# Up to four units of an expert at a time: their up projections first, then their down projections

## The reference

```python
for e in range(N_EXPERTS):
    gu = t @ w_up[e] + b_up[e]
    glu = jnp.minimum(gu[:, 0::2], SWIGLU_LIMIT)
    lin = jnp.clip(gu[:, 1::2], -SWIGLU_LIMIT, SWIGLU_LIMIT)
    act = glu * jax.nn.sigmoid(SWIGLU_ALPHA * glu) * (lin + 1.0)
    y = y + combine[:, e:e + 1] * (act @ w_down[e] + b_down[e])
```

## Time and profile before

| | us |
|---|---|
| median of 3 runs | 1302.47 (1299.08 to 1303.08) |
| the profiled execution | 1299.44 |
| its span, first to last instruction | 1297.7 |
| TensorE matmuls busy | 1116.5 (86% of the span) |
| VectorE busy | 417.1 (32%) |
| ScalarE busy | 219.0 (17%) |
| mean rate over the span | 367 GB/s, 475.76 MB |

### The profile page before, as it was taken

The page is one execution under the profiler, slowest core; times in us unless marked ns, Lnnn a source line. Parts: engine busy times, 40 slices in busy tenths (PEclk is TensorE's granted clock), DMA queues, the critical chain, the costliest instruction groups (busy, mean ns, idle before and its releaser), DMA issues.

```text
span 1297.7 us, 19403 instructions
## 1 busy us (share of the span) xinstructions
PE 1116.5 (86%) x7944; PEld 480.3 (37%) x7944; DVE 417.1 (32%) x1144; ACT 219.0 (17%) x461; POOL 42.2 (3%) x75
## 2 busy tenths in 40 slices
PE   6999998899989556669999667979679797999996
PEld 5864466788533111113333112323213231333331
DVE  1489988641142111112232111322112121232231
ACT  1121023630131000001112100111001110111210
POOL 2000000055000000000000000000000000000000
PEclk9999999999989988889999879998989798999998
DMA  9997771356859999999999999999999999599997
GB/s 327 361 373 300 261 258 65 131 169 219 327 229 428 427 427 428 428 427 428 428 428 427 427 427 427 425 427 427 427 428 428 427 428 428 233 422 423 424 428 312
DMA packets 65561, 475.76 MB, mean 367 GB/s; under 512 B 6329, under 2 KB 18942, under 8 KB 38878
## 3 DMA queue, kind: packets, MB, share of 16 engines
q1 hardware_dynamic: 61844, 471.36, 88.5%
q0 software_dynamic: 816, 1.97, 0.6%
q10 hardware_dynamic: 2842, 1.56, 0.4%
HBM read 473.03 MB, written 1.05 MB: 365 GB/s over the span
## 4 chain that ended last, share of the span: by engine, by line
PE 56%; DMA 33%; DVE 4%; ACT 3%; SPq 3%; issue 1%; ACTq 0%; another core or an unknown queue 0%; DVEq 0%
DMA weights<-in_w_up 19%; PE bank L1549 16%; DMA weights<-in_w_down 14%; PE bank L1577 9%; PE bank L1279 6%; PE bank L1286 5%; PE bank L1491 5%; SPq L458 3%; PE bank L1222 2%; PE bank L1478 2%; PE bank L1271 2%; PE bank L1424 2%; DVE weights L854 2%; PE bank L1498 1%; PE bank L1192 1%; ACT buf_d L768 1%
## 5 line engine op out<-in xcount | busy, mean ns | idle before, releaser
L1549 PE MATMUL bank<-weights,buf_d 128*32 128x512 f32 x3008 | 391.6, 667 | 135.9 <-DMA weights<-in_w_up 135.9
L1549 PEld LDWEIGHTS bank<-weights,buf_d 128*32 128x32 f32 x3008 | 96.2, 116 | 407.6 <-DMA weights<-in_w_up 205.7
L1577 PE MATMUL bank<-weights,buf_d 128*32 128x512 f32 x1504 | 173.6, 596 | 11.5 <-DMA weights<-in_w_down 8.3
L1163 DVE TENSOR_SCALAR u_conv<-bank 128x256 f32<-128x256 f32 x47 | 20.0, 425 | 455.9 <-PE bank L1549 455.9
L764 ACT ACTIVATE u_conv<-u_conv 128x256 f32<-128x256 f32 x47 | 19.6, 416 | 665.6 <-DVE u_conv L1163 665.6
L1491 PE MATMUL bank<-buf_d 64*128 64x512 f32 x384 | 99.9, 640 | 0.9 <-DVE buf_d L1175 0.9
L854 DVE SCALAR_TENSOR_TENSOR weights<-u_conv,weights 128x256 f32<-128x256 f32 x240 | 97.7, 479 | 0.5
L1577 PEld LDWEIGHTS bank<-weights,buf_d 128*32 128x32 f32 x1504 | 42.8, 109 | 108.5 <-issue 74.5
L1279 PE MATMUL bank<-weights,buf_d 128*128 128x512 f32 x192 | 82.9, 593 | 0.0
L1175 DVE TENSOR_TENSOR buf_d<-bank,u_conv 128x512 f32<-128x512 f32 x47 | 32.5, 692 | 144.9 <-PE bank L1577 144.9
L1491 PEld LDWEIGHTS bank<-buf_d 64*128 64x128 f32 x384 | 35.3, 199 | 74.8 <-issue 74.8
(11 more groups left out here) (273 smaller groups left out, 823.3 us busy)
## 6 DMA issues: line engine op xcount, KB each, us to landing
weights<-in_w_up SPq DMA_DIRECT2D x128, 2048.0 KB, 34.1
weights<-in_w_down SPq DMA_DIRECT2D x64, 2048.0 KB, 36.9
weights<-in_w_in SPq DMA_DIRECT2D x10, 2048.0 KB, 14.1
weights<-in_w_ada SPq DMA_DIRECT2D x8, 2048.0 KB, 18.2
weights<-in_w_ada SPq DMA_DIRECT2D x8, 1024.0 KB, 11.5
weights<-in_w_in SPq DMA_DIRECT2D x8, 512.0 KB, 10.4
weights<-in_w_in SPq DMA_DIRECT2D x4, 1024.0 KB, 12.9
weights<-in_w_conv_out SPq DMA_DIRECT2D x2, 2048.0 KB, 11.6
```

Source lines behind the costliest of these rows:

```text
L1549: ins = t.matmul(UP[SLOTS * g:SLOTS * g + SLOTS, :], xgT[:, r, SLOTS * j:SLOTS * j + SLOTS], up_group(w[:, r, :], g), start=False, stop=(j ...
L1577: ins = t.matmul(DOWN[rows, :], actT[:, r, at:at + SLOTS], w[:, g, r, NB * i:NB * i + NB], start=(r == 1 and h == 0 and g == 0), stop=(h = ...
```

## The change

The units of an expert go in runs of up to four (QUEUE). Within a run all up parts come first, one behind the other, and then all down parts. TensorE's up part holds the bias rows, c0 and c1, the gather of the next unit, c2, the transposes of the gathered tokens, c3. Its down part holds the transposes of pickw and of act, the combine of the previous unit, the bias rows and c4 and c5. The products lin of a run wait in four tiles of 256 columns (queue); ScalarE copies them one by one into act in the down part. The sigmoid is written over its own input glu, and so starts behind the product of lin and glu. sel exists twice, for up and for down. apply_mod goes in two halves, four operations for two, the first half after c1 is used. VectorE's and ScalarE's programs get a copy of the loops for every expert, as TensorE's has. The core of the diff:

```diff
+QUEUE = 4
...
-        act = area_q[:, 512:768]
-        actT = area_q[:, 768:1024].rearrange("p (r s) -> p r s", r=2)
-        xg = area_q[:, 1024:1280]
+        queue = area_q[:, 512:512 + QUEUE * T]
+        actT = area_q[:, 1792:2048].rearrange("p (r s) -> p r s", r=2)
+        xg = area_q[:, 1536:1792]
...
-        oe = area_q[:, 1536:2048]
+        oe = area_k[:, 848:848 + NB]
...
-        sel = area_k[0:3 * EXPERTS, 576:576 + SLOTS // 2].bitcast(BF16)
+        sel_up = area_k[0:3 * EXPERTS, 576:576 + SLOTS // 2].bitcast(BF16)
+        sel_down = area_k[0:3 * EXPERTS, 2146:2146 + SLOTS // 2].bitcast(BF16)
         glu = area_k[:, 592:848]
         comb4 = glu.rearrange("p (k e) -> p k e", e=EXPERTS)
-        lin = area_k[:, 848:1104]
-        sg = area_k[:, 1104:1360]
+        act = glu
...
+        up_pairs = UP[:, :].rearrange("p (f two) -> p f two", two=2)
+
+        def expert_end(eng, e):
+            return eng.value_load(unit_ends[0:1, e:e + 1], min_val=e + 1, max_val=UCOLS - 1)
+
+        def run_end(first, end):
+            n = (end - first).with_bounds(min_val=1, max_val=T // SLOTS)
+            more = ((n - 1) >> 2).with_bounds(min_val=0, max_val=1)
+            return (first + (n - more * (n - QUEUE)).with_bounds(min_val=1, max_val=QUEUE)).with_bounds(min_val=1, max_val=UCOLS - 1)
+
+        def queued(u, first):
+            return queue[:, bass.ds((u - first).with_bounds(min_val=0, max_val=QUEUE - 1) * T, T)]
...
             g.memset(oe, 0.0).then_inc(oe_ready, 1)
+            g.memset(queue[:, 3 * T:4 * T], 0.0).then_inc(up_read, 1)
...
-            count = act_e.value_load(unit_ends[0:1, EXPERTS - 1:EXPERTS], min_val=EXPERTS, max_val=UCOLS - 1)
-            with act_e.Fori(0, count) as u:
-                act_e.wait_ge(glu_ready, u + 1)
-                s.activation(sg, glu, ACT.Sigmoid, scale=ALPHA).then_inc(sg_ready, 1)
+
+            def up_part(u, first):
                 act_e.wait_ge(gathered, u + 2)
                 s.copy(xg, GX[:, 0:T]).then_inc(xs_ready, 1)
+                act_e.wait_ge(glu_read, u + 1)
+                s.activation(glu, glu, ACT.Sigmoid, scale=ALPHA).then_inc(sg_ready, 1)
+                act_e.wait_ge(act_ready, u + 1)
+
+            def down_part(u, first):
+                s.copy(act, queued(u, first)).then_inc(act_kept, 1)
                 act_e.wait_ge(t_done, u + 1)
                 s.copy(actT, TR[:, 0:T].rearrange("p (r s) -> p r s", r=2)).then_inc(actT_ready, 1)
+                act_e.wait_ge(cmb_read, u + 1)
                 s.copy(Cmb, TR[:, T:2 * T]).then_inc(cmb_ready, 1)
+
+            begin = 0
+            for e in range(EXPERTS):
+                end = expert_end(act_e, e)
+                with act_e.Fori(begin, end, QUEUE) as first:
+                    last = run_end(first, end)
+                    with act_e.Fori(first, last) as u:
+                        up_part(u, first)
+                    with act_e.Fori(first, last) as u:
+                        down_part(u, first)
+                begin = end
...
-            def apply_mod(link, at, done):
...
+            def apply_mod(link, at, half, done):
+                pair = slice(2 * half, 2 * half + 2)
...
+                link(v.tensor_tensor(to, seen, xg_scale[:, :, pair].unsqueeze(3).to_broadcast(places), ALU.mult), at)
+                v.tensor_tensor(to, to, xg_shift[:, :, pair].unsqueeze(3).to_broadcast(places), ALU.add).then_inc(done, 1)
 
             dve.wait_ge(xt_done, 1)
-            apply_mod(lambda ins, at: step(ins), 0, xm_ready)
+            apply_mod(lambda ins, at: step(ins), 0, 0, xm_low)
+            apply_mod(lambda ins, at: step(ins), 0, 1, xm_ready)
...
+            def make_sel(dst, u, ready):
+                v.tensor_copy(dst, onehot[:, bass.ds(u, 1)].to_broadcast([3 * EXPERTS, SLOTS])).then_inc(ready, 1)
+
+            def make_pickw(u):
...
+
+            make_pickw(0)
+            PER_UNIT = 2
+
+            def up_part(u, first):
+                def link(ins, k):
+                    ins.then_inc(u_step, 1)
+                    dve.wait_ge(u_step, u * PER_UNIT + k)
+
+                lin = queued(u, first)
                 make_pick(u + 1)
+                dve.wait_ge(xt_done, u + 2)
+                dve.wait_ge(chunk_used[1], u + 1)
+                apply_mod(link, 1, 0, xm_low)
                 dve.wait_ge(UP_DONE, u + 1)
-                pairs = UP[:, :].rearrange("p (f two) -> p f two", two=2)
-                v.tensor_scalar(glu, pairs[:, :, 0], LIMIT, None, ALU.min).then_inc(glu_ready, 1)
-                link(v.tensor_scalar(lin, pairs[:, :, 1], LIMIT, -LIMIT, ALU.min, ALU.max), 1)
+                v.tensor_scalar(glu, up_pairs[:, :, 0], LIMIT, None, ALU.min).then_inc(glu_ready, 1)
+                v.tensor_scalar(lin, up_pairs[:, :, 1], LIMIT, -LIMIT, ALU.min, ALU.max).then_inc(up_read, 1)
+                apply_mod(link, 2, 1, xm_ready)
                 dve.wait_ge(glu_ready, u + 1)
-                link(v.scalar_tensor_tensor(lin, lin, 1.0, glu, ALU.add, ALU.mult), 2)
+                dve.wait_ge(up_read, u + 2)
+                v.scalar_tensor_tensor(lin, lin, 1.0, glu, ALU.add, ALU.mult).then_inc(glu_read, 1)
+                make_sel(sel_up, u + 1, sel_up_ready)
                 dve.wait_ge(sg_ready, u + 1)
-                v.tensor_tensor(act, lin, sg, ALU.mult).then_inc(act_ready, 1)
-                dve.wait_ge(gathered, u + 2)
-                make_sel(u + 1)
-                dve.wait_ge(xt_done, u + 2)
-                apply_mod(link, 3, xm_ready)
-
+                v.tensor_tensor(lin, lin, glu, ALU.mult).then_inc(act_ready, 1)
+
+            def down_part(u):
+                dve.wait_ge(t_done, u + 1)
+                make_pickw(u + 1)
                 dve.wait_ge(DOWN_DONE, u + 1)
                 v.tensor_tensor(oe, DOWN[:, :], gate2, ALU.mult).then_inc(oe_ready, 1)
+                make_sel(sel_down, u + 1, sel_down_ready)
+
+            begin = 0
+            for e in range(EXPERTS):
+                end = expert_end(dve, e)
+                with dve.Fori(begin, end, QUEUE) as first:
+                    last = run_end(first, end)
+                    with dve.Fori(first, last) as u:
+                        up_part(u, first)
+                    with dve.Fori(first, last) as u:
+                        down_part(u)
+                begin = end
...
-            def unit(e, u):
+            def up_rows(e, j):
+                w = up_chunk(e, j)
+                pe.wait_ge(w_full[chunk_slot(e, j)], chunk_landed(e, j))
+                for r in range(2):
+                    for g in range(GROUPS):
+                        ins = t.matmul(UP[SLOTS * g:SLOTS * g + SLOTS, :], xgT[:, r, SLOTS * j:SLOTS * j + SLOTS],
+                                       up_group(w[:, r, :], g), start=False, stop=(j == 3 and r == 1))
+                ins.then_inc(chunk_used[j], 1)
+
+            def up_part(e, u):
+                pe.wait_ge(xm_low, u + 1)
+                pe.wait_ge(sel_up_ready, u + 1)
+                pe.wait_ge(up_read, u + 1)
+                bias_rows(UP, range(GROUPS), sel_up, up_bias)
+                up_rows(e, 0)
+                up_rows(e, 1)
                 pe.wait_ge(xm_ready, u + 1)
-                pe.wait_ge(sel_ready, u + 1)
-                bias_rows(UP, range(GROUPS), up_bias)
-                for j in range(4):
-                    w = up_chunk(e, j)
-                    pe.wait_ge(w_full[chunk_slot(e, j)], chunk_landed(e, j))
-                    for r in range(2):
-                        for g in range(GROUPS):
-                            ins = t.matmul(UP[SLOTS * g:SLOTS * g + SLOTS, :], xgT[:, r, SLOTS * j:SLOTS * j + SLOTS],
-                                           up_group(w[:, r, :], g), start=False, stop=(j == 3 and r == 1))
-                    ins.then_inc(chunk_used[j], 1)
-
-                pe.wait_ge(oe_ready, u + 1)
-                pe.wait_ge(cmb_ready, u + 1)
-                combine()
-                pe.wait_ge(units_ready, 2)
-                bias_rows(DOWN, (0, 2), down_bias)
                 pe.wait_ge(pick_ready, u + 2)
                 gather()
+                up_rows(e, 2)
+                pe.wait_ge(xs_ready, u + 2)
+                transpose_halves(GX, T, xg).then_inc(xt_done, 1)
+                up_rows(e, 3)
+
+            def down_part(e, u):
                 pe.wait_ge(pickw_ready, u + 1)
+                pe.wait_ge(cmb_ready, u + 1)
                 for tt in range(TT):
                     t.transpose(TR[:, T + P * tt:T + P * tt + P], pickw[:, tt, :], ident[:])
-                pe.wait_ge(act_ready, u + 1)
+                pe.wait_ge(act_kept, u + 1)
                 transpose_halves(TR, 0, act).then_inc(t_done, 1)
-                pe.wait_ge(xs_ready, u + 2)
-                transpose_halves(GX, T, xg).then_inc(xt_done, 1)
-
+                pe.wait_ge(oe_ready, u + 1)
+                combine(read=cmb_read)
+                pe.wait_ge(sel_down_ready, u + 1)
```

(25 more changed lines are left out.)

21 lines of the change are left out of this document (5 added, 16 removed).

## The result

The changed kernel takes 1336.5 us (median of four runs, 1333.8 to 1338.9) against 1301.0 before (four runs), a ratio of 1.027, with 1.024 to 1.030 as its 95% interval. The forecast was 1331, slower with a chance of 0.92. Direction, mechanism and range held; the long wait and the unit's own time were a little too small, and two statements about the DMA were wrong.

The account below looks back on a forecast made before the run. Expert weight transfers and TensorE were all but level, with TensorE becoming the bound from unit 34: 33.7 us of waits plus 9 of lower clock less 14.1 gained gives +28.6, hence 1331 us; range 1315 to 1350.

Parts of the forecast that it names:

- (a): Joint from up part to down part, once per expert: TensorE waits 3.1 us ahead of the act transposes, seven times.
- The drain of the Trainium skill: Full drain after each VectorE operation would add about 9 us; the sum instead used clamps measured 0.34 us apart.
- (b): Joint from up part to up part: TensorE waits 1.9 us for the UP bank and sel_up, six times.
- (c): Joint from down part to down part: the combine waits 0.1 us for the previous unit's oe, six times.
- The clock: TensorE's lower clock level behind each 3.1 us wait: 1.3 us each, seven times, 9 us; short waits charged nothing.
- The gain of 14.1 us: From unit 34 on, TensorE free of weight waits would reach the tail at 1276.4 us instead of 1290.5.
- No new hole there: Ahead of unit 34, units 8 to 15: TensorE falls back 22 us, the ring of chunks holds 25 us ahead.
- ACT_TABLE_LOAD: ScalarE's table load, 1.28 us per unit, priced at nothing: expected beneath the third and fourth chunk's rows.
- (2): Rival: the same TensorE waits, but the clock holds; +19.6 us, 1322 us, chance 0.22.
- (3): Rival: more exposed at the joints, or low clock behind short waits too; 1341 to 1350 us, chance 0.13.
- (4): Rival: waits are short and removing the transfer hole wins, long wait under 1.2 us; 1298 or 1288 us, chance 0.06.
- (5): Rival: waits at their floors of 2.0 and 0.9 us with a full clock; 1308 us or somewhat less, chance 0.04.

Follow-up runs that it names:

- fill_wait: Changed kernel plus twenty useless TensorE transposes of the identity in the long wait ahead of each run's down parts; 1324.0 us.
- all_three: Changed kernel with the combine ahead of the wait for act, sel_up made ahead of the clamps and apply_mod's high half behind the second multiply; 1312.1 us.
- the second profile: The changed kernel run and profiled once more, nothing altered; 1336.1 us in one run.
- peeled: Changed kernel with each run's first down part written out, combine first, transposing straight from the queue; sel_up early, apply_mod's high half late; 1306.6 us.
- comb_first: Changed kernel with the previous unit's combine ahead of the wait for act and its transposes in TensorE's down part; 1323.6 us.
- hi_late: Changed kernel with the high half of apply_mod moved from between the clamps and the product to behind the last multiply; 1337.7 us.
- before_loops: Kernel before, order of work unchanged, with the change's per-expert loops, value_load and run_end on VectorE, ScalarE and TensorE; 1302.0 us, ratio 1.0002.
- sel_early: Changed kernel with VectorE making sel_up for the next unit ahead of the clamps instead of behind the product; 1338.5 us.
- peeled_two: As peeled, but a run holds at most two units instead of four; 1305.0 us, ratio 1.0021.

## Why the prediction was right or wrong

**What bounds the kernel, and who takes over: right.** Behind unit 34 TensorE waits for no weights in the changed kernel. Its stretch is 185.1 + 35.5 + 13.2 us; fill_wait takes most of the last term away, all_three more than half of the second. The span grew by 10.9 us more than forecast (39.5 for 28.6): 4.9 ahead of unit 34, 1.8 in the waits, 4.2 in the rest.

**(a), the long wait: 3.1 forecast, 3.28 measured.** Up to the second multiply each step sat where the sum had it: lin at T + 0.35 (0.34), the high half at + 0.68 and + 0.99 (0.68 and 1.00), product + 1.20 (1.21), sigmoid + 1.65 (1.67), multiply + 2.10 (2.13). The step that was mis-sized is ScalarE's way from the multiply to the copy: the copy started 0.60 us after the multiply's end, where I had 0.04 + 0.25. Hand-over, the way out of one loop and into the next, and the address of the queued tile all lie in it, and no run takes them apart.

**The drain of the Trainium skill, weighed against the row.** The changed kernel's independent operations start 0.33 to 0.35 us apart (L1204, L1205, L1161), and the chain came out where the sum by the row had it. The Trainium skill ("VectorE: DVE Perf Modes", section "The DRAIN you can't avoid") has the full drain as its main case and a start earlier than that as the exception; the trace shows the exception alone, and 9 us more of drains would have been wrong.

**(b) and (c): 1.9 forecast, 1.87 measured; 0.1 forecast, 0.2 measured.**

**The clock: mechanism right, size near.** 7 x 1.3 = 9 us forecast; of the rest of 13.2 us the clock is 10.7 (against fill_wait), in the second profile 8.3 of 10.7. The forecast lies between two profiles of the same kernel, so how well it sits is in part luck. A smaller term that I missed is in the rest too: a unit at full clock takes 8.71 + 6.35 = 15.06 us without its waits, from up part to up part and down part to down part, where I used 14.91; 0.15 x 12 = 1.8. The clock is 1.2 to 1.5 us for each long wait on average, 0 in the expert that begins at 1207 us (35.54 = 2 x 15.06 + 3.28 + 1.87 + 0.23) and 1.7 in the single-unit one (20.03 - 15.06 - 3.28). The 1.9 us waits, which I charged nothing, were rightly charged nothing: no fall of the clock comes behind one.

**The gain of 14.1 us: the number held, the reason given did not.** I wrote that without the hole the last chunk is there before 1276. The hole doesn't vanish under the new order. It moves, 14.2 us of it to 1140 to 1160 us in the changed kernel, since c4 and c5 of the four-unit expert are held until its last down part; peeled shows 9 us of it and, with TensorE's waits short, a last chunk that lands no sooner than before (1290.4 us, before 1288.5; I had it ahead of 1276). "In small pieces, not in one hole", the sign I named for the stretch behind 1130 us, was wrong with it. In the changed kernel this was hidden behind TensorE's 48.7 us of waits and clock, so it didn't touch the sum. It means that the order had less than 14.1 us to win even with free joints: peeled needs 201.7 us for the stretch, before 199.2.

**"No new hole there", ahead of 1090 us: wrong by 2 to 4 us of transfers.** I had weighed units 8 to 15 against the ring with waits only, and not with the lower clock. The small hole at 700 to 740 us is there, and it is gone in comb_first, in hi_late and with filler. Most of the 4.9 us isn't it, though: 4.2 are the later start of the stage, which no term of mine had and which differs from execution to execution.

**ACT_TABLE_LOAD: priced at nothing, and right for another reason.** I had it fall beneath the third chunk's rows. In fact it is gone from the loop: 47 loads, one per unit, before (60.3 us); in the changed kernel one load each at the two lines:

```profile
L782 ACT ACT_TABLE_LOAD x1 | 1.3, 1283 | 0.7 <-issue 0.7
L784 ACT ACT_TABLE_LOAD x1 | 1.3, 1283 | 0.0
```

The new order of the work isn't what removed them. before_loops has the old order in the new loops, and one load at its sigmoid (L772) too, with ScalarE busy for 160.2 us instead of 219.0 and the kernel's time unchanged: the loads cost nothing, as ScalarE was idle there anyway.

**Loops and register work: at nothing, right** (before_loops, ratio 1.0002) wherever they aren't in a joint; in one they may be the 0.3 us that (a) lacked.

**The rivals.** (2), the clock holds, was refuted here, and fill_wait shows its world: 1324.0, forecast 1322. (3), 1341 to 1350, begins 4.5 us above the measured 1336.5, and the forecast of 1331 lies 5.5 below, so the number alone doesn't choose between them. The waits do: 35.5 us of them for 33.7, and no lower clock behind the short ones. (4) and (5) needed a long wait under 1.2 or of 2.0 us; all_three has 1.1 us long waits and lands at 1312, (5)'s neighbourhood, still behind before, since its order uncovers the copies of actT.

## What to carry to other kernels

Count what the interleaving hides before regrouping loops: in the old order the activation chain of 1.7 us lay beneath a combine and a gather, in the new one it, a copy and the hand-overs lay bare 7 times in the last 13 units, and that cost more than the transfer hole that was to be won (and that stayed). When a ring's slots are freed by groups of work, ask for every chunk of the group when its last reader ends; a larger group may free the first chunks sooner and the last ones later. And where TensorE is the bound, price a wait of some 3 us at a third to a half more than its length, for the lower clock behind it (here 3.3 + 1.2 to 1.5), and shorten the longest wait first.

## What the runs showed of the hardware

The clock fell only behind the long waits. From unit 34 to the last down result, in the kernels profiled, every fall began late in a wait of 2.6 to 3.3 us or in the work right behind it, and none came behind one of 1.9 us or less. With twenty transposes in the long wait, or with the combine in it, none came in this stretch but one each in peeled and peeled_two, behind a wait of 2.6 us for weights. Not every long wait brings a fall: five of seven did in each profile of the changed kernel, seven of seven in sel_early, where six other waits had been cut from 1.9 to 1.0 us. So shorter waits elsewhere can leave the clock lower for longer, 37.5 us against 23.9 and 17.1; what decides it from wait to wait, these runs don't tell. The price was 0.40 to 0.49 us for each us at the lower level.

A sigmoid and copies by ScalarE in one loop over all units came with a table load per unit (47 of 1.28 us); the same operations in the same order, in one pair of loops for each expert, came with a single one (before_loops). And the time ahead of the experts' stage differs between two profiles of one and the same kernel by 2.75 us (376.07 and 373.32).
